# Attention slots of a two-layer decoder step: page copies inside the suffix work, projection products in two halves, narrow weights and masks moved

## What is computed

```
z = einsum(q, k) * 64**-0.5 + bias
log_beta = log_sigmoid(z)
log_1m   = where(k_pos < q_pos, log_sigmoid(-z), 0)
rest     = cumsum(log_1m, reverse) - log_1m
w        = where(k_pos < q_pos, exp(log_beta + rest), 0);   out = w @ v
```

## Time and profile before

| what | value |
|---|---|
| median of the runs shown | 3548.84 us (3548.02 to 3550.63) |
| the profiled execution's own time | 3551.58 us |
| its span, first to last instruction | 3549.8 us |
| mean granted clock of TensorE in it | 0.912 of 2.4 GHz |
| the attention of layer 1 | about 1597.9 to 2547.0 us of the span |

### The profile page before, as it was taken

How to read it: one execution, slowest core, us unless ns; L and a number is a source line. 1 busy time by engine, 2 the same in 40 slices (tenths; PEclk the granted TensorE clock), 3 DMA queues, 4 the chain that set the end, 5 groups by cost and what they waited for, 6 DMA issues and landing times.

```text
span 3549.8 us, 52658 instructions
## 1 busy us (share of the span) xinstructions
PE 3062.0 (86%) x20085; PEld 2820.6 (79%) x20085; DVE 1620.3 (46%) x1899; ACT 882.1 (25%) x1505; POOL 938.6 (26%) x461
## 2 busy tenths in 40 slices
PE   7888886959999999967888888888686999999994
PEld 6787885949999999957666666666586999999994
DVE  3554544662332212363665666556675233221236
ACT  3233231031101101023454444545403100100102
POOL 3221211323343333332121121111032333333330
PEclk9898987979999999978898998989797999999997
DMA  3010110101111111102333233332210111111111
GB/s 100 25 35 25 30 36 19 36 18 47 42 48 41 47 42 47 34 25 86 94 99 100 90 120 90 96 102 90 79 47 18 47 42 47 41 42 47 47 36 49
DMA packets 311740, 195.87 MB, mean 55 GB/s; under 512 B 12842, under 2 KB 309495, under 8 KB 311610
## 3 DMA queue, kind: packets, MB, share of 16 engines
q1 hardware_dynamic: 302522, 189.63, 17.8%
q10 hardware_dynamic: 9088, 4.52, 0.4%
HBM read 178.70 MB, written 15.40 MB: 55 GB/s over the span
## 4 chain that ended last, share of the span: by engine, by line
PE 76%; DVE 13%; ACT 5%; issue 4%; DMA 0%; POOL 0%; SPq 0%; ACTq 0%; DVEq 0%; POOLq 0%
PE bank L1403 61%; DVE E L1194 3%; PE bank L1654 2%; PE bank L1416 2%; PE bank L1630 2%; DVE LS L1312 2%; PE bank L1567 2%; PE bank L1642 1%; DVE R L1307 1%; PE bank L1581 1%; DVE R L1318 1%; ACT WTK L757 1%; DVE KTP L1215 1%; ACT E L788 1%; PE bank L1610 1%
## 5 line engine op out<-in xcount | busy, mean ns | idle before, releaser
L1403 PE MATMUL bank<-XH,WH 128*128 128x352 f32 x3264 | 1087.2, 333 | 36.2 <-ACT Q L644 10.0
L1403 PE MATMUL bank<-XH,WL 128*128 128x352 f32 x3264 | 1066.2, 327 | 0.0
L1403 PE MATMUL bank<-XL,WH 128*128 128x352 f32 x3264 | 1065.1, 326 | 0.0
L560 POOL TENSOR_TENSOR WH<-RAW,zero 128x1024 fp32r<-128x1024 f32 (+1 forms) x204 | 393.2, 1927 | 2400.1 <-PE bank L1403 2291.4
L1403 PEld LDWEIGHTS bank<-XH,WH 128*128 128x128 f32 x3264 | 630.2, 193 | 61.8 <-issue 47.9
L1403 PEld LDWEIGHTS bank<-XH,WL 128*128 128x128 f32 x3264 | 631.7, 194 | 0.0
L1403 PEld LDWEIGHTS bank<-XL,WH 128*128 128x128 f32 x3264 | 628.3, 192 | 0.0
L1403 PE MATMUL bank<-HH,WH 128*128 128x352 f32 x1440 | 473.5, 329 | 56.9 <-DVE HL L1353 32.3
L563 POOL TENSOR_TENSOR WL<-RAW,WH 128x1024 fp32r<-128x1024 f32 (+1 forms) x204 | 512.6, 2513 | 16.0
L1403 PE MATMUL bank<-HH,WL 128*128 128x352 f32 x1440 | 469.1, 326 | 0.0
L1403 PE MATMUL bank<-HL,WH 128*128 128x352 f32 x1440 | 468.3, 325 | 0.0
(11 more groups left out here) (277 smaller groups left out, 3162.8 us busy)
## 6 DMA issues: line engine op xcount, KB each, us to landing
PG<-in_cache_k_dram SPq DMA_DIRECT2D x256, 128.0 KB, 2.2
PG<-in_cache_v_dram SPq DMA_DIRECT2D x256, 128.0 KB, 2.2
RAW<-in_ffn_w_gate_dram SPq DMA_DIRECT2D x44, 512.0 KB, 3.8
RAW<-in_ffn_w_up_dram SPq DMA_DIRECT2D x44, 512.0 KB, 3.8
RAW<-in_ffn_w_down_dram SPq DMA_DIRECT2D x32, 512.0 KB, 3.8
RAW<-in_c_w_in_dram SPq DMA_DIRECT2D x28, 512.0 KB, 4.6
RAW<-in_ab_w_in_dram SPq DMA_DIRECT2D x24, 512.0 KB, 3.9
RAW<-in_ffn_w_down_dram SPq DMA_DIRECT2D x16, 384.0 KB, 3.3
```

The source lines that it names most:

```text
L560: nc.gpsimd.tensor_tensor(WH[slot][:, 0:kb, :], RAW[slot][:, 0:kb, :], zero[:].to_broadcast([P, kb, P]), ALU.add).then_inc(w_split, 1)
L1403: last = t.matmul(bank[:, 0:CW], w[slot][:, k, :], x[:, k, CH[c]], start=n == 0, stop=n == 3 * kb - 1)
```

## The change

- **DVE.** `exponent` is cut in two: `suffix_sums` (scan) and `exponent` (subtraction). A slot's page copies of places three, four and five now stand after the first head's scan, after its subtraction and after the second head's scan.
- **PE.** From slot 1 on a product is issued as two halves of 12 matmuls, one before and one after the turn of the last block's weights. In slot 0 the whole product moves ahead of the second part of the logits, behind two turns of value tokens. S is put into bank 4 instead of bank 7, and the next Q no longer waits for S to be read.
- **Value steps.** `V_SPOTS` has the same number in each slot, at other places.
- **ACT.** In slots 2, 4 and 6 the copies of the narrow block's turned weights come between the first and second head's exp and ln. The evacuation of a product comes after the copies of the turned weights (slot 0: before the exp).
- **Start.** The wait for all masks goes from PE, ACT and DVE; the turn of WTN and its copy move into slot 0 of pair 0 (bank 6). On POOL the second pair of weight splits goes ahead of the ten selections.

```
-        V_SPOTS = [(), (1, 0, 1, 0, 1)] + [(0, 0, 1, 0, 1)] * 5 + [(1, 0, 1, 0, 1), ()]
+        V_SPOTS = [(), (0, 0, 1, 1, 1), (1, 0, 0, 1, 0), (0, 0, 0, 1, 1), (1, 0, 0, 1, 0), (0, 0, 0, 1, 1), (1, 0, 0, 1, 0),
+                   (0, 0, 1, 1, 1), ()]
 # POOL, attention_pool
+                split_pair("c", KD, 1)
                 for q in range(2):
 ...
-                splits("c", len(C_TILE) // 2, KD, 1)
+                splits("c", len(C_TILE) // 2, KD, 2)
 # ACT, attention_act
-                act.wait_ge(at_pool, 14)
 # ACT, pair
+                        if p == 0:
+                            for x in items:
+                                item(*x, banks[7])
                         if p < NPOS:
-                            for h in range(2):
-                                log1p_exp(hp, p, h)
-                        for x in items:
-                            item(*x, banks[7])
+                            log1p_exp(hp, p, 0)
                         if p == 0:
                             value_tokens(hp, 2)
 ...
+                        elif p < NPOS and WIDE[p]:
+                            weights_turned(hp, p - 1, 0)
+                        if p < NPOS:
+                            log1p_exp(hp, p, 1)
                         if p == 1:
                             for b in range(3):
                                 key_tokens(hp, b)
+                        if p == NPOS or not WIDE[p]:
+                            weights_turned(hp, p - 1, 0)
                         if p >= 1:
-                            weights_turned(hp, p - 1, 0)
+                            for x in items:
+                                item(*x, banks[4 if x[0] == "S" else 7])
 # DVE, attention_dve
-                dve.wait_ge(at_pool, 14)
-                dve.wait_ge(cap_mm, 1)
-                v.tensor_copy(CAPQ[:], banks[4][:, 0:NS]).then_inc(cap_ready, 1)
+                def new_token_cap():
+                    dve.wait_ge(cap_mm, 1)
+                    v.tensor_copy(CAPQ[:], banks[6][:, 0:NS]).then_inc(cap_ready, 1)
 # DVE, pair
                             copies()
+                            suffix_sums(hp, p, 0)
+                            copies()
                             exponent(hp, p, 0)
                             copies()
+                            suffix_sums(hp, p, 1)
+                            copies()
                             exponent(hp, p, 1)
-                            copies()
-                            copies()
+                            if hp + p == 0:
+                                new_token_cap()
 # PE
-                pe.wait_ge(at_pool, 14)
-                t.transpose(banks[4][:, 0:NS], WTN[:], ident[0:NS, 0:NS]).then_inc(cap_mm, 1)
+                def new_token_cap():
+                    pe.wait_ge(at_pool, 14)
+                    freed(ITEMS[9])
+                    t.transpose(banks[6][:, 0:NS], WTN[:], ident[0:NS, 0:NS]).then_inc(cap_mm, 1)
 ...
+                def next_products(items, k0, k1):
+                    for x in items:
+                        if x[0] == "S":
+                            if k0 == 0:
+                                item(*x, banks[4])
+                            continue
+                        if k0 == 0:
+                            freed([y for y in ITEMS[:ITEMS.index(x)] if y[0] != "S"][-1])
+                        item(*x, banks[7], k0, k1)
 # PE, pair
+                        if p == 0:
+                            value_tokens(hp, 1)
+                            next_products(items, 0, KD)
                         fill()
                         if p < NPOS and WIDE[p]:
                             logits(hp, p, 1)
-                        if p == 0:
-                            value_tokens(hp, 1)
                         fill()
-                        for x in items:
-                            freed(ITEMS[ITEMS.index(x) - 1])
-                            item(*x, banks[7])
+                        if p >= 1:
+                            next_products(items, 0, KD // 2)
 ...
                         if p >= 1:
                             turn(hp, p - 1, 0)
+                            next_products(items, KD // 2, KD)
                         fill()
```

More of the change, by code:

```diff
@@ L724, in queries @@
                     e = hp % 2
+                    if hp < 2:
+                        act.wait_ge(at_pool, 3)
                     for h in range(2):
@@ L1181, in logits_in @@
                         if part == 0:
+                            if hp + p == 0:
+                                dve.wait_ge(at_pool, 4)
                             if p >= 2:
@@ L1187, in logits_in, with suffix_sums @@
                             v.tensor_scalar(z, bank, bias, ZCAP, ALU.add, ALU.min).then_inc(z_ev, 1)
-                def exponent(hp, p, h):
-                    u, w = 2 * NPOS * hp + 2 * p + h + 1, WIDTH[p]
-                    z, e = ZS[WIDE[p]][h], ES[h]
+                def suffix_sums(hp, p, h):
+                    u, w, e = 2 * NPOS * hp + 2 * p + h + 1, WIDTH[p], ES[h]
                     dve.wait_ge(e_ln, u)
@@ L1195, in exponent @@
                                          ALU.mult, ALU.add).then_inc(suffix, 1)
+                def exponent(hp, p, h):
+                    u, w, z, e = 2 * NPOS * hp + 2 * p + h + 1, WIDTH[p], ZS[WIDE[p]][h], ES[h]
                     dve.wait_ge(suffix, u)
@@ L1510, in attention_pe, with item @@
                 pe.wait_ge(ln_cent, 6)
-                pe.wait_ge(at_pool, 14)
-                t.transpose(banks[4][:, 0:NS], WTN[:], ident[0:NS, 0:NS]).then_inc(cap_mm, 1)
+                def new_token_cap():
+                    pe.wait_ge(at_pool, 14)
+                    freed(ITEMS[9])
+                    t.transpose(banks[6][:, 0:NS], WTN[:], ident[0:NS, 0:NS]).then_inc(cap_mm, 1)
                 def freed(x):
                     pe.wait_ge(q_lo if x[0] == "Q" else c_free, FREED[x])
-                def item(kind, c, hp, bank):
+                def item(kind, c, hp, bank, k0=0, k1=KD):
                     n = C_TILE[kind, hp]
-                    if c == 0 or kind == "S" or kind == "Q" and c == 2:
+                    if k0 == 0 and (c == 0 or kind == "S" or kind == "Q" and c == 2):
                         pe.wait_ge(w_split, 2 * n + 5)
                     if kind != "S":
-                        product(n % 2, KD, c, XH, XL, bank)
+                        for k in range(k0, k1):
+                            for m, (w, x) in enumerate(((WH, XH), (WL, XH), (WH, XL))):
+                                last = t.matmul(bank[:, 0:CW], w[n % 2][:, k, :], x[:, k, CH[c]],
+                                                start=k == 0 and m == 0, stop=k == KD - 1 and m == 2)
+                        if k1 == KD:
+                            last.then_inc(d_mm, 1)
                         return
@@ L1649, in values @@
                         pe.wait_ge(po_ev, NPOS * hp + p)
+                    if part == 0 and hp + p == 0:
+                        pe.wait_ge(cap_ready, 1)
                     pe.wait_ge(t_ev, TURN[hp, p, part, 1] + 1)
@@ L1683, in pair @@
                             logits(hp, p, 1)
-                        if p == 0:
-                            value_tokens(hp, 1)
                         fill()
-                        for x in items:
-                            freed(ITEMS[ITEMS.index(x) - 1])
-                            item(*x, banks[7])
+                        if p >= 1:
+                            next_products(items, 0, KD // 2)
                         if p == 0:
                             value_tokens(hp, 2)
+                            if hp == 0:
+                                new_token_cap()
                             for b in range(2 * odd):
```

2 lines of the change are left out of this document (1 added, 1 removed).

## The result

Five runs of the changed kernel took 3526.15 to 3532.47 us, median 3530.91, beside 3548.84 before: ratio 0.9946, 95% interval 0.9931 to 0.996. So it is faster, by about 18 us of the 56 forecast. The profiled execution took 3526.15 (span 3524.4); it is the quickest of the five, so its rows show some 5 us less than the median.

What follows compares the result with a forecast made beforehand. The prediction took PE's waits for DVE's and ACT's copies, their echo in the clock, and PE's own work as the bound. Gains of 66.4 us less 10 for the clock left 56, giving 3493 us, range 3462 to 3536.

Steps and rivals of the forecast that it cites:

- Slots 2 and 3 of pair 2: Even pair: page steps start about 8.5 and 11.8 us in beside POOL's split; gain 4 of 32.5 us.
- slots 4 and 5: Even pairs gain 4.7 us, about 1 us of copy waits staying; odd pairs gain 2.0 of 19.7 us.
- The start: First V product runs once XL's first third is ready, not after POOL's selections: gain 3 us, bounds 2 and 4.3.
- the wait for KTP: Sign that the forecast is right: PE's wait for KTP is halved.
- odd slots 6 to 8: Bank 4 removes PE's wait for S; 0.8 left for ACT's delayed second exp, gain 5.4 us, bounds 2.7 and 6.2.
- slots 0 and 1: V0 ahead of the second logits: odd pairs lose 1.2 us (gain 1 to loss 3), even pairs gain 0.3.
- the end of the even pair: Slots 6 to 8, already busy at full clock: gain 2.2 of 2.6 idle us, bounds 0 and 2.6.
- The first rival: DVE's copies ahead of the second subtraction lengthen the chain in even pairs' wide slots: 24 us gained, 3525 us; chance 0.16.
- pair 7 at 0: Pair 7 carries no products and keeps DVE's old order, so its change is 0.
- The clock falls under the halves: Rival: halves cut by turns run at the lower clock, 84 us more against 56 gained, 3577 us; chance 0.11.
- The waits only change places: Rival: the chain is the bound everywhere, products move among waits of equal length, 3549 us; chance 0.07.
- The 10 us set aside for the clock: Allowance for waits that stay in slots 0 to 3: one half product per pair at the lower clock, 7 x 1.4.

Runs made afterwards that it cites:

- act_wide_back: Changed kernel, but in slots 2, 4 and 6 ACT again takes both heads' exp and ln before copying the narrow block's turned weights: 3511.85 us.
- vspots_back: Changed kernel with the old places of the value steps, all else as changed: 3511.23 us.
- v0_back_odd: Changed kernel with V0 behind the second logits again in odd pairs, and ACT taking both exps first in slot 0: 3522.54 us.
- v0_back_tail: Changed kernel with V0 behind the second logits in all pairs, ACT's exps first in every slot, and DVE's old order in even pairs' slot 7: 3474.82 us.
- copies_alone: Kernel before the change with only DVE's page copies moved between scan and subtraction: 3502.83 us.
- copies_v0: Kernel before the change with the page copies moved and V0 ahead of the second logits, evacuated by ACT before the exps: 3546.62 us.
- copies_tail: Same as copies_alone, but with DVE's old order in slot 7 of the even pairs: 3491.06 us.
- halves_odd: Same as v0_back_tail, but with halves of products in odd pairs only and undivided products in even pairs: 3461.54 us.
- whole: Changed kernel with every product undivided again, all 24 matmuls ahead of the turn of the last block's weights: 3540.70 us.

## Why the prediction was right or wrong

**Right.** Slots 2 and 3 of pair 2 gained 3.2 us (forecast 4; 4.0 to 6.5 in the other even pairs) with both page steps where the working put them; slots 4 and 5 gained 5.1 (4.7). Slots 2 and 3 of the odd pair stayed (0.1), slots 4 and 5 gained 2.2 (2.0). The start gained 3.6 (3). S in bank 4 and the early start were undone in no kernel by themselves, so these two are read from rows alone. Of the signs named beforehand, the clock of 1.00 in slots 4 and 5 and the first product right behind XL came; the wait for KTP fell by two fifths instead of half. As SBUF goes, the Trainium skill (SBUF — State Buffer, Who interferes with whom) holds for these rows: a subtraction that starts with POOL's WH took 2.80 us where the undisturbed one took 1.09, longer by 1.7, nearly the whole 1.89 of WH.

**Wrong 1: odd slots 6 to 8,** a gain of 5.4 that was a loss of 0.8. The failed step of the prediction is "ACT's second exp now stands behind the copies of the small turned block, so I leave 0.8". The wait was seen and priced as ACT's own. What the second exp holds up was not followed: DVE's scan and subtraction, QL behind them, bank 7 behind QL, and PE's next product behind the bank. act_wide_back shows it: with ACT's old order the stretch took 28.4 us, 4.7 less than before and near the 5.4 forecast, and 19 us came back in all. The new value places had a part in it, since vspots_back brings back as much with ACT's order kept; the prediction put no price on them there. Bank 4 did take away the wait for S.

**Wrong 2: slots 0 and 1.** In the odd pair 4.8 us were lost, beyond the bound of 3; I took 1.2. Some 3 of them are V0's: with V0 behind the second logits again the two slots took 30.2 us instead of 32.9 (v0_back_odd). The rest comes over from the end of the pair before, which is wrong 3: v0_back_tail shortens the same slots from 29.8 to 26.9. For V0 the place and the wait for bank 7 were right; the term counted V0's length and let part return in slot 1. It left out ACT's VNS, a second wait of 2.61 us behind the late logits. In the even pair the 0.3 of gain came out as a loss of 0.3, but as a sum of two things that the working had not sized so: 4.9 us that the copies give in slots 0 and 1 (copies_alone), and as much that V0 takes (copies_v0). Undone in all pairs, V0's move is worth 19 us here, and 44 in a kernel with undivided products.

**Wrong 3: the end of the even pair,** slots 6 to 8, +0.3 where 2.2 were to be gained, with 2.3 more in slot 0 of the next pair. The step "2.2 of the 2.6 idle us" looked at PE alone. The first rival (copies lengthen the chain) had the mechanism, with the place wrong: in the other slots the copies' move paid on balance, which fits its own counter-argument. In slot 7 no later block covers the later weights: the sample chain, QL and the next pair wait there. It costs 15 us in all (v0_back_tail), and 12 in copies_alone (copies_tail).

**Wrong 4: pair 7 at 0.** It lost 5.8 us, 4.3 of them in slots 0 and 1 (24.9 before, 29.2 after). The reason given for the 0, DVE's old order, passes over ACT's order, the value places, and the end of pair 6. The last can cost that much: copies_alone and copies_tail have the code of before in pair 7, differ only in slot 7 of the even pairs, and took 28.9 and 25.2 us for its first two slots. Pair 7's second logits in copies_alone:

```profile
2416.00 0.79 PE L1635 MATMUL bank<-KH,QH 64*128 64x512 f32 x2 [4.89 <-DVE Z L1184]
```

and in copies_tail:

```profile
2405.24 0.50 PE L1639 MATMUL bank<-KH,QH 64*128 64x512 f32 x2 [2.49 <-DVE Z L1184]
```

PE waits for the first mask, which DVE makes only behind the sample chain and QL; in the kernel after it waits 4.23 us there. The whole pair took 91.2 us at a clock of 0.79 in copies_alone and 86.9 at 0.76 in copies_tail, so the clock does not make this difference. The rest is not settled: v0_back_tail and halves_odd have the same code in pair 7 too and took 91.1 and 86.0 us, with PE busy for 61.90 us at 0.72 in the one and for 57.81 at 0.76 in the other; there the clock goes with the difference, and no run shows which of the two leads.

**The rivals.** *The clock falls under the halves* did not come: whole shows the opposite sign. But the halves' worth in the even pairs was assumed, not bounded: there they cost, 13 us with what follows in the odd pairs and in pair 7 (v0_back_tail to halves_odd), while they help in odd pairs. The Trainium skill (TensorE: Matmul & The Clock Gate, Why this matters for your kernels) advises for matmuls with M below 512 to run all k tiles before the next DMA, or the clock swings with each tile. Here the odd pair speaks against running them unbroken (100.2 us with halves, 102.9 without), the even pair for it (111.5 and 108.8). The clock goes the same way (0.93 and 0.90 in the odd pair, 0.95 and 0.98 in the even one), and apart from the 0.9 us beside POOL no run separates it from the waits. *The waits only change places* had the right idea for the four end stretches: 19.3 us behind QL stand where others went.

**The size.** Of the 42 us between ledger and trace, 30 lie in the odd pairs, 6 each in the even pairs and pair 7. The 10 us set aside for the clock did not cover the waits that were missed: behind the 2.83 us for QL, for one, the half product's matmuls stand 0.29 us apart, and 0.16 at the full clock. The total of 3530.91 lies inside the stated range only by the room left for the first rival, around 3525. That it came so near to that figure is luck: the rival's delay made 15 us of the loss, at another place, and ACT's order and V0's place cost 19 us each.

## What to carry to other kernels

When a step on an engine that works in order is delayed, follow the last thing queued behind it, not only the step: here one exp reached a bank and a product three engines on. A step that frees a resource may stand inside a chain as long as a later stage covers the chain's end (46 us gained here); at the last stage, where nothing covers it, put it behind (12 to 15 us). A change of many edits is as many predictions: one edit alone gained 46 us, all together 18, and with two of them undone and two narrowed 87.

## What the hardware showed unexpectedly

DVE and POOL delay each other by who starts first: with POOL 0.41 us ahead, a scan of 1056 columns took 3.70 us and WH 1.89; with the scan 1.13 us ahead, the scan took 2.36 and WH 2.91. So a shift of DVE by 1.5 us cost 3.3 here. And code that is word for word the same (pair 7) took 86.0 to 91.2 us by what stands ahead of it, once at the higher clock in the longer time (91.2 us at 0.79, 86.9 at 0.76) and once at the lower (91.1 at 0.72, 86.0 at 0.76).
